# One core, Trainium2: the input phases of four feed-forward stages by a Strassen scheme, seven block products for eight

## What is computed

```
xp = xp + 0.5 * swiglu(rmsnorm(xp, norm_g[layer, 0]), w_ffn_in[layer, 0], w_ffn_out[layer, 0])
...                      # token mixer
xp = xp + 0.5 * swiglu(rmsnorm(xp, norm_g[layer, 2]), w_ffn_in[layer, 1], w_ffn_out[layer, 1])

def swiglu(h, w_in, w_out):
    gu = h @ w_in
    return (jax.nn.silu(gu[..., :D_FF]) * gu[..., D_FF:]) @ w_out
```

## Time and profile before

| | |
|---|---|
| median of 3 runs | 2457.79 us (2454.14 to 2458.47) |
| the profiled execution | 2459.19 us |
| its span, first to last instruction | 2457.4 us |
| PE busy | 2326.3 us, 95% |
| DVE, ACT, POOL busy | 1099.2, 718.7, 334.3 us |
| mean granted PE clock | 0.974 of full |

### The profile page before, as it was taken

How to read it: one execution, slowest core, us unless ns; L and a number is a source line. 1 busy time by engine, 2 the same in 40 slices (tenths; PEclk the granted TensorE clock), 3 DMA queues, 4 the chain that set the end, 5 groups by cost and what they waited for, 6 DMA issues and landing times. The chain is left out here.

```text
span 2457.4 us, 43360 instructions
## 1 busy us (share of the span) xinstructions
PE 2326.3 (95%) x17356; PEld 2105.0 (86%) x17356; DVE 1099.2 (45%) x1776; ACT 718.7 (29%) x1188; POOL 334.3 (14%) x402
## 2 busy tenths in 40 slices
PE   5999999996899989999999999999998899999997
PEld 5999999775754579999999999999665489999997
DVE  5443444223367645443444442444475734433443
ACT  2221222223145313322322321222254413222220
POOL 1000003000145312000002000003174311000002
PEclk8999999997899989999999999999999999999998
DMA  3332332224320212332332233232213012332331
GB/s 98 91 102 81 91 98 81 78 79 131 130 69 1 69 35 86 94 97 83 94 103 77 87 101 87 86 99 77 78 52 106 1 52 77 93 100 81 93 98 58
DMA packets 327481, 202.48 MB, mean 82 GB/s; under 512 B 11698, under 2 KB 306666, under 8 KB 327322
## 3 DMA queue, kind: packets, MB, share of 16 engines
q1 hardware_dynamic: 323226, 199.10, 27.4%
q10 hardware_dynamic: 4160, 2.10, 0.3%
HBM read 194.65 MB, written 10.70 MB: 84 GB/s over the span
## 5 line engine op out<-in xcount | busy, mean ns | idle before, releaser
L166 DVE TENSOR_TENSOR w_lo<-w_stage,w_hi 128x1024 fp32r<-128x1024 f32 (+1 forms) x268 | 357.3, 1333 | 828.1 <-ACT w_hi L159 828.0
L159 ACT ACTIVATE w_hi<-w_stage 128x1024 fp32r<-128x1024 f32 (+1 forms) x278 | 314.0, 1129 | 752.9 <-PE y_ps L173 344.2
L171 PE MATMUL gate_ps<-h_hi,w_hi 128*128 128x260 f32 x1408 | 401.9, 285 | 17.2 <-DVE h_lo L195 7.5
L173 PE MATMUL gate_ps<-h_hi,w_lo 128*128 128x260 f32 x1408 | 401.1, 285 | 0.0
L172 PE MATMUL gate_ps<-h_lo,w_hi 128*128 128x260 f32 x1408 | 401.0, 285 | 0.0
L171 PE MATMUL up_ps<-h_hi,w_hi 128*128 128x260 f32 x1408 | 398.2, 283 | 0.0
L173 PE MATMUL up_ps<-h_hi,w_lo 128*128 128x260 f32 x1408 | 398.2, 283 | 0.0
L171 PE MATMUL y_ps<-a_hi,w_hi 128*128 128x260 f32 x1408 | 398.1, 283 | 0.0
L172 PE MATMUL up_ps<-h_lo,w_hi 128*128 128x260 f32 x1408 | 397.9, 283 | 0.0
L173 PE MATMUL y_ps<-a_hi,w_lo 128*128 128x260 f32 x1408 | 397.6, 282 | 0.0
L172 PE MATMUL y_ps<-a_lo,w_hi 128*128 128x260 f32 x1408 | 397.6, 282 | 0.0
(11 more groups left out here) (437 smaller groups left out, 3239.9 us busy)
## 6 DMA issues: line engine op xcount, KB each, us to landing
w_stage<-w_ffn_in SPq DMA_DIRECT2D x176, 512.0 KB, 3.8
w_stage<-w_ffn_out SPq DMA_DIRECT2D x64, 704.0 KB, 4.5
...
```

What stands on the lines that cost most here:

```text
L159: act.activation(e.w_hi[slot][:, 0:cols], e.w_stage[slot][:, 0:cols], ACT.Copy).then_inc(e.hi_done, 1)
L166: dve.tensor_tensor(e.w_lo[slot][:, 0:cols], e.w_stage[slot][:, 0:cols], e.w_hi[slot][:, 0:cols].bitcast(F32), ALU.subtract).then_inc(e.lo ...
L171: pe.matmul(out, w_hi, x_hi, start=first, stop=False)
L173: return pe.matmul(out, w_lo, x_hi, start=False, stop=last)
```

## The change

For each strip the gate tile and the up tile (two column blocks), the even and odd chunks k (two inner blocks) and the two token halves form a 2x2 by 2x2 block product. Eight block products become seven of 4 chunks x 3 passes = 12 matmuls each: 84 matmuls in a strip in place of 96. The matmuls keep their shape, 128x128 weights against 260 tokens.

What is new around them:

- Four weight combinations in each strip, 128x512 each, on POOL (`combine`): even up + odd up; that minus even gate; even up minus even gate; odd gate minus the second.
- The split works on seven pieces of 128x512 instead of two tiles of 128x1024: seven on ACT (`piece_hi`), six on DVE and one on POOL (`piece_lo`).
- Seven token operands instead of four: `Terms`, with DVE and ACT instructions for each pair of chunks (`pair_act`, `pair_dve`), in the output phases and projections ahead of a stage, and at the program's start.
- The products come out in seven PSUM banks, one each. Two are copied out by ACT (`keep_first`, `keep_third`), five are added in by DVE (`first_gate`, `second_sum`, `third_sum`, and the first instruction of `finish_gate` and of `finish_up`), and POOL makes two more sums (`sums_of_strip`). Then the scaling by `rs` on DVE, now from SBUF; Silu, product and split as before.
- PE waits for the piece of its product (`piece_lo`, `last_lo`) and until that product's bank of the strip before has been read.
- The output phase writes into the same PSUM tensor `acc`, so that the second half's input phase starts only when the last addition to `x` is done.
- The norm's sum at the program's start is accumulated by PE (`start_statistics`) instead of DVE.
- Some SBUF of the mixers (`ot`, `pages` and others) is taken from the new staging tensor `big`.

The core of the diff:

```diff
+def combine(e, pool, s):
+    mixed = [flat(e.mixed[:, i * PIECE:(i + 1) * PIECE]) for i in range(3)]
+    a11, a12, a21, a22 = (raw_of(e, s, side, odd) for side in range(2) for odd in range(2))
+    pool.wait_ge(e.strip_in[s.par], s.landed())
+    if not s.first:
+        pool.wait_ge(e.piece_lo, s.count(6, -2))
+    pool.tensor_tensor(mixed[0], a21, a22, ALU.add).then_inc(e.mix_done, 1)
+    pool.wait_ge(e.mix_done, s.count(4, 1))
+    pool.tensor_tensor(mixed[1], mixed[0], a11, ALU.subtract).then_inc(e.mix_done, 1)
+    pool.tensor_tensor(a21, a21, a11, ALU.subtract).then_inc(e.mix_done, 1)
+    pool.wait_ge(e.mix_done, s.count(4, 2))
+    if not s.first:
+        pool.wait_ge(e.piece_lo, s.count(6, 0))
+    pool.tensor_tensor(mixed[2], a12, mixed[1], ALU.subtract).then_inc(e.mix_done, 1)
...
+def piece_hi(e, act, s, j):
+    if not s.first:
+        act.wait_ge(e.product_done, s.count(7, j - 6))
+        if s.c == 0 and j not in (2, 3, 4):
+            act.wait_ge(e.unit_used, out_start(e, s) - (j < 2))
+    if j in (0, 1, 6):
+        act.wait_ge(e.strip_in[s.par], s.landed())
+    else:
+        act.wait_ge(e.mix_done, s.count(4, (2, 1, 3, 4)[j - 2]))
+    act.activation(high_of(e, s, j), source_of(e, s, j), ACT.Copy).then_inc(e.piece_hi, 1)
+def piece_lo(e, eng, s, j):
+    eng.wait_ge(e.piece_hi, s.count(7, j + 1))
+    eng.tensor_tensor(low_of(e, s, j), source_of(e, s, j), high_of(e, s, j).bitcast(F32), ALU.subtract)\
+       .then_inc(e.last_lo if j == 6 else e.piece_lo, 1)
...
+def pair_dve(e, dve, terms, norm, i):
+    even_dve(e, dve, terms, norm, i)
+    even_lo_of(e, dve, terms, i)
+    turned_dve(e, dve, terms, norm, i)
+    odd_lo_of(e, dve, terms, i)
+    turned_lo_of(e, dve, terms, i)
...
+            def sums_of_strip(s):
+                pool.wait_ge(e.second_sum, s.count(1, 1))
+                pool.wait_ge(e.third_kept, s.count(1, 1))
+                if not s.first:
+                    pool.wait_ge(e.act_ready, s.count(1, 0))
+                pool.tensor_tensor(gate_t[:, 1, :], kept[:, 1, :], kept[:, 2, :], ALU.add).then_inc(e.fourth_done, 1)
+                pool.wait_ge(e.third_sum, s.count(1, 1))
+                pool.tensor_tensor(up_t[:, 1, :], up_t[:, 0, :], kept[:, 2, :], ALU.add).then_inc(e.up_second, 1)
+            def strip(s):
+                then = s.next()
+                combine(e, pool, then)
+                sums_of_strip(s)
+                piece_lo(e, pool, then, 6)
             if at_start:
...
+            def product(s, j, operand, waits=None, adds=1):
+                if j == 6:
+                    pe.wait_ge(e.last_lo, s.count(1, 1))
+                else:
+                    pe.wait_ge(e.piece_lo, s.count(6, j + 1))
+                if not s.first:
+                    pe.wait_ge(read[j], s.count(1, 0))
+                (hi, lo, b), high, low = operand, high_of(e, s, j), low_of(e, s, j)
+                for k in range(PAIRS):
+                    if waits is not None:
+                        pe.wait_ge(waits, tn + k + 1)
+                    m = three_passes(pe, acc[:, j, 0:TH], high[:, k, :], low[:, k, :], hi[:, k, b, :], lo[:, k, b, :],
+                                     k == 0, k == PAIRS - 1)
+                if adds:
+                    m.then_inc(e.product_done, adds)
+            A, B = (e.a_terms_hi, e.a_terms_lo), (e.b_terms_hi, e.b_terms_lo)
+            operands = ((*A, 0), (*A, 2), (*B, 0), (*A, 1), (*B, 1), (*A, 3), (*B, 2))
+            read = (e.first_kept, e.gate_first, e.second_sum, e.third_kept, e.third_sum, e.gate_second, e.strip_read)
+            def strip(s):
+                for j in range(7):
...
+            def start_statistics():
+                for k in range(KC):
+                    pe.wait_ge(e.start_squared, k + 1)
+                    for half in range(2):
+                        m = pe.matmul(stat_ps[:, half, 0:TH], e.ones[:, :], start_sq[k % 2][:, half * TH:(half + 1) * TH],
+                                      start=k == 0, stop=k == KC - 1)
...
+            def strip(s, after):
+                then = s.next()
+                keep_first(s)
+                if after:
+                    silu_of(s, 1)
+                piece_hi(e, act, then, 0)
+                piece_hi(e, act, then, 1)
+                if not after and not at_start and s.half == 2 * n:
+                    root()
+                piece_hi(e, act, then, 2)
+                keep_third(s)
+                piece_hi(e, act, then, 3)
+                if after:
+                    a_hi_of(s, 1)
+                for j in (4, 5, 6):
+                    piece_hi(e, act, then, j)
...
+            def first_gate(s):
+                dve.wait_ge(e.product_done, s.count(7, 2))
+                dve.wait_ge(e.first_kept, s.count(1, 1))
+                if not s.first:
+                    dve.wait_ge(e.act_ready, s.count(1, 0))
+                dve.tensor_tensor(gate_t[:, 0, :], kept[:, 0, :], acc[:, 1, 0:TH], ALU.add).then_inc(e.gate_first, 1)
+            def second_sum(s):
+                dve.wait_ge(e.product_done, s.count(7, 3))
+                if not s.first:
+                    dve.wait_ge(e.fourth_done, s.count(1, 0))
+                dve.tensor_tensor(kept[:, 1, :], kept[:, 0, :], acc[:, 2, 0:TH], ALU.add).then_inc(e.second_sum, 1)
+            def third_sum(s):
+                dve.wait_ge(e.product_done, s.count(7, 5))
+                dve.wait_ge(e.second_sum, s.count(1, 1))
+                dve.tensor_tensor(up_t[:, 0, :], kept[:, 1, :], acc[:, 4, 0:TH], ALU.add).then_inc(e.third_sum, 1)
+            def finish_gate(s, back):
+                dve.wait_ge(e.product_done, s.count(7, 6 - 7 * back))
+                dve.wait_ge(e.fourth_done, s.count(1, 1 - back))
+                dve.tensor_tensor(gate_t[:, 1, :], gate_t[:, 1, :], acc[:, 5, 0:TH], ALU.add).then_inc(e.gate_second, 1)
+                dve.wait_ge(e.gate_second, s.count(1, 1 - back))
+                dve.tensor_tensor(gate_t[:, :, :], gate_t[:, :, :], rs2, ALU.mult).then_inc(e.gate_scaled, 1)
+            def finish_up(s, back):
+                dve.wait_ge(e.product_done, s.count(7, 7 - 7 * back))
+                dve.wait_ge(e.up_second, s.count(1, 1 - back))
+                dve.tensor_tensor(up_t[:, 0, :], up_t[:, 0, :], acc[:, 6, 0:TH], ALU.add).then_inc(e.strip_read, 1)
+                dve.wait_ge(e.strip_read, s.count(1, 1 - back))
+                dve.tensor_tensor(up_t[:, :, :], up_t[:, :, :], rs2, ALU.mult).then_inc(e.up_scaled, 1)
+            def act_of(s, back):
+                dve.wait_ge(e.silu_done, s.count(1, 1 - back))
+                dve.wait_ge(e.up_scaled, s.count(1, 1 - back))
+                dve.wait_ge(e.a_lo_done, s.count(1, 1 - back))
+                dve.tensor_tensor(act_t, up_t[:, :, :], gate_t[:, :, :], ALU.mult).then_inc(e.act_ready, 1)
+            def a_lo_of(s, back):
+                dve.wait_ge(e.a_hi_done, s.count(1, 1 - back))
+                f = s.at() - back
+                dst, hi = (a_lo[:, f, :], a_hi[:, f, :]) if isinstance(f, int) else (a_lo[:, ds(f, 1), :], a_hi[:, ds(f, 1), :])
+                dve.tensor_tensor(dst, act_t.rearrange("p a t -> p (a t)"), hi.bitcast(F32), ALU.subtract).then_inc(e.a_lo_done, 1)
+            def strip(s, after):
+                then = s.next()
+                if after:
+                    finish_gate(s, 1)
...
+            def strip(s, after):
+                then = s.next()
+                if after:
+                    finish_gate(s, 1)
+                    finish_up(s, 1)
+                    act_of(s, 1)
+                piece_lo(e, dve, then, 0)
+                first_gate(s)
+                piece_lo(e, dve, then, 1)
+                second_sum(s)
+                piece_lo(e, dve, then, 2)
+                if after:
+                    a_lo_of(s, 1)
+                piece_lo(e, dve, then, 3)
+                third_sum(s)
+                piece_lo(e, dve, then, 4)
+                piece_lo(e, dve, then, 5)
+                if not after and s.half == 2 * n:
                     dve.wait_ge(e.rms_done, e.norm_n + 1)
                     dve.reciprocal(e.rs[:, :], e.rms[:, :]).then_inc(e.rs_done, 1)
                     dve.wait_ge(e.rs_done, e.norm_n + 1)
-                gate_of(b, 0, F, half == 0)
...
+                s = Strip(0, FH - 1, 2 * n + half)
+                finish_gate(s, 1)
+                finish_up(s, 1)
+                act_of(s, 1)
+                first_gate(s)
+                second_sum(s)
                 split_lo(e, dve, out0[half], 0, FH * P)
-                gate_of(b + 2 * (FH - 1), 0, F + FH - 1, False)
-                strip_of(b + 2 * (FH - 1), 0, F + FH - 1, FH - 1)
+                a_lo_of(s, 1)
+                third_sum(s)
```

More of the change, by code:

```diff
@@ new lines, in piece_of, with out_start, high_of, low_of @@
+def piece_of(e, s, j, split, slots):
+    if j in (2, 3, 4):
+        return flat(split[:, (j - 2) * PIECE:(j - 1) * PIECE])
+    at, first = j % 5 * PIECE, out_start(e, s) % 2
```

(82 more changed lines are left out.)

498 lines of the change are left out of this document (312 added, 186 removed).

## The result

The changed kernel takes **2597.66 us** (median of 4, 2595.66 to 2598.11) for 2458.13 before on the same chip: 1.0571 times as long, interval [1.0555, 1.0587]. Its profiled span is 2595.9 us, 138.5 more than before.

The account below looks back on a forecast made before the run. PE bounded the kernel before; DVE and POOL taking turns would bound the changed strips. Terms of +119 us on the 2457.4 us span gave 2576, 2577 us as a median; range 2465 to 2650.

Parts of the forecast that it names:

- my two residues: Input strips: what is left of an instruction behind the other engine's, 0.55 us on DVE (520 columns), 1.15 on POOL.
- the bound 0: Input strips: DVE's sums from PSUM share nothing with a busy POOL; the other bound was 1.5 us a strip.
- 0.9 us of empty queue: Input strip: time when neither DVE nor POOL wants two SBUF tensors, around `second_sum` and `third_sum`; strip 13.4 us.
- the shared sum of 12.45: Input strip: 10 x 0.55 + 5 x 1.15 + 2 x 0.6 us of DVE and POOL instructions taking turns.
- DVE's own load of "8.1": Input strip: DVE's ten instructions on two SBUF tensors and five sums from PSUM, together 8.1 us, fitting in 10.08.
- 4 x 4.1 us, done near 45.5: Start of ffn0: DVE builds four pairs of terms beside POOL's eight squares; +4 us beyond the +9.9.
- output phases and clock: Around output phases: second output tile's split +10 us, second half's wait for the last `x` +4, lower PE clock +4.
- the reciprocal's 3.4: ffn1 to ffn3: DVE's reciprocal, between piece 5 and `finish_gate`, costs its 3.40 us length; +10 us in all.
- Packs better: Input strips: the 0.9 us of empty queue vanish, strips take 12.45 us, kernel 2508 us; chance 0.13.
- less sharing: Input strips: DVE and POOL share less than whole instructions; faster below 11.7 us a strip, 2367 without sharing; chance 0.13.
- sums from PSUM queue too: Input strips: DVE's PSUM sums also wait for POOL, or hand-overs cost more; strips 14.5 us, kernel 2656; chance 0.06.
- clock stays low: Input strips: PE's matmuls stay 0.217 us apart, strip 18.2, kernel beyond 2800 us; chance of over 2650: 0.05.

Follow-up runs that it names:

- the 64-column stage: Kernel before with short stages appended after its end; in this one 64-column DVE instructions run beside 512-column POOL ones: six pass in 7.36 us.

## Why the prediction was right, and where not

- **Right: the mechanism and the strip.** Whole instructions in turn, 1.60 us a pair measured for the 1.70 of my two residues (0.55 and 1.15); sums from PSUM outside it (0.41; the bound 0 was the one to take); strip 13.30 for 13.4; second halves +10.3 for +9.9. The Trainium skill, "SBUF — State Buffer", section "SBUF: two separate sides", calls it an exclusive lock that is held for the whole instruction; the 64-column stage agrees (six in 7.36 us). PE waits for `w_lo`, as said, for 2.30 and 1.30 us in the two strips shown; it is busy for 83 and 90%, not three quarters, and DVE for 99%, not 95%.
- **Right for a reason too simple.** I added 0.9 us of empty queue to the shared sum of 12.45. The runs show DVE never idle and a sum of waits instead. In this kernel both give the same; in the run with the sums on DVE they part by 1.1 us a strip. DVE's own load of "8.1" does not follow from its terms either, which make 7.8 (10 x 0.61 + 5 x 0.34); the runs give 8.05.
- **Mis-sized: the start of ffn0**, +26.2 for 13.9. The failing step was "4 x 4.1 us, done near 45.5". In the changed kernel:

```profile
40.63 2.03 DVE L471 TENSOR_TENSOR turned_lo<-kept,turned_hi 128x780 fp32r<-128x780 f32 x1
42.59 1.48 DVE L439 SCALAR_TENSOR_TENSOR gate_t<-x,gain,gate_t 128x260 f32<-128x260 f32 x1
50.19 0.49 DVE L439 SCALAR_TENSOR_TENSOR gate_t<-x,gain,gate_t 128x260 f32<-128x260 f32 x1 [1.43 <-ACT gate_t L407]
54.39 0.97 DVE L471 TENSOR_TENSOR turned_lo<-kept,turned_hi 128x780 fp32r<-128x780 f32 x1 [0.32 <-ACT turned_hi L432]
```
  A pair goes back and forth between ACT and DVE over one set of buffers. DVE begins the four pairs at 25.81, 32.47, 42.59 and 50.19 us, and the terms end at 55.4, ten us later than I had. So the pairs take 6.7, 10.1, 7.6 and 5.2 us, none of them 4.1. In the second, DVE's rows are stretched beside POOL's squares and the combinations for the next strip (`turned_lo` 2.03 us for 0.97 in the fourth pair); I had counted the squares there and not the combinations. Ahead of the fourth pair the root of the norm stands on ACT. The run with POOL's part cut short shows 9.8 us that the start costs without the longer strips; working by pairs gave 4.3 of it back, and the rest was not taken apart.
- **Mis-sized: the projections**, 17.8 for 8. I had bounds of 0 and 12 for both; the pair's chain holds back the `x` behind it and the five pieces stand ahead of the last `x`, whose wait PE shows:

```profile
994.84 0.69 DVE L1654 TENSOR_TENSOR x<-nsa_y_ps,x 128x520 f32<-128x520 f32 x1
```
```profile
996.00 0.56 PE L198 MATMUL acc<-h_hi,w_hi 128*128 128x260 f32 x1 [6.36 <-PEq L1580]
```
  Reordering only moved it. It is work that DVE has to do before the stage can go on; that this is the whole cause is argued, not shown.
- **Too high: output phases and clock**, 12.1 for 18. **First halves of ffn1 to ffn3:** beyond a second half's +10.3 they gained 3.9, 4.2 and 0.2 where I had the reciprocal's 3.4. The reciprocal does cost about that: in the changed kernel a first half is 5.9 to 6.1 us longer than a second one in all three stages; with POOL's part cut short, where PE is the bound, it is 2.4. The 3.5 between them fits the reciprocal. The small gain in ffn3 comes from the kernel before: there its first half was 3.6 us longer than that of ffn1, because its first 48 matmuls had a granted clock of 0.50 for part of the way (2050 to 2053 us) and took 9.4 us; in ffn1 they had 1.00 and took 5.7. The changed kernel starts both stages at a clock near 0.5 (0.52 from 996 to 1000 us, 0.53 from 2160.55 to 2164).
- **Rivals.** "Packs better", "less sharing", "sums from PSUM queue too" and "clock stays low" all fall: 13.30, the pair of 1.60, 0.41, and a granted clock of 1.00 in the second window: it fell behind the wait of 2.30 us and came back within the strip.
